# Moving three weight splits of GpSimd from ahead of the first expert gather to between the fourth and eighth

## The reference, cut to what matters

```python
q = (ht @ w_query).astype(jnp.float32).reshape(t_, PEER_HEADS, 2, PEER_HALF)
s1 = jnp.einsum('thd,hkd->thk', q[:, :, 0], sub_keys_1)   # and s2 with the other half
v1, i1 = lax.top_k(s1, PEER_TOPK)
...
idx = jnp.take_along_axis(cand_idx, pos, axis=-1)
gate = jax.nn.softmax(top_s, axis=-1)
...
u_sel = jnp.take(expert_down, ib, axis=0)
act = jnp.einsum('tkd,td->tk', u_sel, hb)
w = gb * jax.nn.gelu(act, approximate=False)
v_sel = jnp.take(expert_up, ib, axis=0)
return jnp.einsum('tk,tkd->td', w, v_sel)
```

## Time and profile before

| What | Value |
|---|---|
| Median of 3 runs | 3589.9 us (3586.92 to 3591.99) |
| Profiled execution, its own time | 3589.78 us |
| Span of that execution in the trace | 3588.0 us |
| PE busy | 3245.0 us, 90% of the span |
| POOL busy | 2185.1 us, 61% |
| DVE busy | 1754.7 us, 49% |
| ACT busy | 1332.6 us, 37% |
| All transfers | 936.79 MB, mean 261 GB/s |

### The profile page before, as it was taken

One profiled execution on the slowest core, in us unless ns is written; L12 is line 12 of the kernel. 1 busy time (PEld: TensorE's weight loads), 2 busy tenths in 40 slices (PEclk: granted clock), 3 DMA queues, 4 the chain that ended last, 5 costly groups with the idle time before them and its releaser, 6 DMA issues.

```text
span 3588.0 us, 38848 instructions
## 1 busy us (share of the span) xinstructions
PE 3245.0 (90%) x13642; PEld 2303.8 (64%) x13642; DVE 1754.7 (49%) x2582; ACT 1332.6 (37%) x2038; POOL 2185.1 (61%) x1216
## 2 busy tenths in 40 slices
PE   9999999996787788777877789999999999999998
PEld 7888878874343234222322338888888888878887
DVE  7998264238666447544744552222232133335444
ACT  6777576442111011000100014444444444445553
POOL 2021767876445444455555537887788778878665
PEclk9999999998999999999999999999999999999999
DMA  7455545669999999999999985555554445555444
GB/s 229 134 151 143 168 147 162 211 197 366 419 419 420 421 418 420 421 420 421 421 417 421 417 345 194 175 173 170 169 175 170 171 168 178 172 184 173 150 145 169
DMA packets 232765, 936.79 MB, mean 261 GB/s; under 512 B 28176, under 2 KB 31248, under 8 KB 166032
## 3 DMA queue, kind: packets, MB, share of 16 engines
q0 software_dynamic: 76288, 538.74, 36.3%
q1 hardware_dynamic: 152848, 391.96, 33.3%
q10 hardware_dynamic: 3456, 3.77, 0.3%
HBM read 927.04 MB, written 2.10 MB: 259 GB/s over the span
## 4 chain that ended last, share of the span: by engine, by line
PE 65%; DMA 25%; DVE 5%; POOL 1%; issue 1%; DVEq 1%; ACT 1%; ACTq 0%; SPq 0%; POOLq 0%
PE products L675 41%; DMA arena<-peer_up_in,arena 22%; PE products L2185 8%; PE products L1540 6%; DMA arena<-peer_down_in,arena 3%; DVE arena L2140 1%; POOL arena L2131 1%; PE products L1210 1%; PE products L2747 1%; PE products L1316 1%; PE products L2709 1%; PE products L1233 1%; DVE weights_low L634 1%; DVE arena L2166 0%; PE products L1222 0%
## 5 line engine op out<-in xcount | busy, mean ns | idle before, releaser
L634 POOL TENSOR_TENSOR weights_low<-arena,weights_high 128x1024 fp32r<-128x1024 f32 x484 | 1187.2, 2461 | 370.6 <-ACT weights_high L622 324.5
L2185 PE MATMUL products<-arena 128*128 128x512 f32 x1984 | 936.9, 618 | 290.2 <-DMA arena<-peer_up_in,arena 234.4
L622 ACT ACTIVATE weights_high<-arena 128x1024 fp32r<-128x1024 f32 x604 | 637.8, 1059 | 979.8 <-PE products L675 949.9
L675 PE MATMUL products<-weights_high,input_high 128*128 128x512 f32 x2416 | 985.2, 408 | 14.9 <-DVE weights_low L634 13.3
L675 PE MATMUL products<-weights_low,input_high 128*128 128x512 f32 x2416 | 946.6, 392 | 0.0
L675 PE MATMUL products<-weights_high,input_low 128*128 128x512 f32 x2416 | 944.3, 391 | 0.0
L2185 PEld LDWEIGHTS products<-arena 128*128 128x128 f32 x1984 | 369.6, 195 | 839.3 <-issue 418.9
L2140 DVE SCALAR_TENSOR_TENSOR arena<-arena 128x2048 f32<-128x2048 f32 x256 | 585.8, 2292 | 519.7 <-DMA arena<-peer_down_in,arena 519.3
L2131 POOL DMA_INDIRECT arena<-peer_up_in,arena x256 | 389.1, 1520 | 522.4 <-PE products L2185 500.2
L675 PEld LDWEIGHTS products<-weights_high,input_high 128*128 128x128 f32 x2416 | 455.8, 189 | 111.2 <-DVE weights_low L634 15.2
L675 PEld LDWEIGHTS products<-weights_low,input_high 128*128 128x128 f32 x2416 | 454.8, 188 | 98.7
(11 more groups left out here) (367 smaller groups left out, 3070.5 us busy)
## 6 DMA issues: line engine op xcount, KB each, us to landing
arena<-dsa_in SPq DMA_DIRECT2D x320, 512.0 KB, 3.5
arena<-w_in_in SPq DMA_DIRECT2D x128, 512.0 KB, 3.9
arena<-mla_wide_in SPq DMA_DIRECT2D x88, 512.0 KB, 3.5
arena<-w_attn_o_in SPq DMA_DIRECT2D x32, 512.0 KB, 4.3
arena<-w_out_in SPq DMA_DIRECT2D x32, 512.0 KB, 4.0
arena<-peer_w_query_in SPq DMA_DIRECT2D x32, 512.0 KB, 10.1
arena<-dsa_w_out_in SPq DMA_DIRECT2D x32, 512.0 KB, 3.8
arena<-glu_w_b_in SPq DMA_DIRECT2D x16, 512.0 KB, 3.7
```

The costliest lines, as they stand in the source:

```text
L622: nc.scalar.activation(w_hi[:, u % RING, :, at], ring[:, u % RING, :, at], ACT.Copy).then_inc(hi_made, 1)
L634: ops.tensor_tensor(w_lo[:, u % RING, :, at], ring[:, u % RING, :, at], w_hi[:, u % RING, :, at].bitcast(F32), op=ALU.subtract).then_inc(l ...
L675: mm = nc.tensor.matmul(PS[:, bank(b) + t, 0:width], x[:, x0 + n, at], y, start=n == 0 and m == 0, stop=n == len(parts) * PK - 1 and m == 2)
L2185: mm = nc.tensor.matmul(PS[:, SUM_BANKS[q]], diag[:, d % ROWS], row[:, q * NC:(q + 1) * NC], start=h % 2 == 0 and n == 0, stop=bool(last))
```

## The change

GpSimd no longer makes the low halves of parts 0 to 2 of the second query slab ahead of its first gather, nor that of part 3 after the fourth gather. It makes the one of part 0 after the fourth gather, of part 1 after the fifth, of part 2 after the sixth and of part 3 after the seventh.

```diff
             pool.wait_ge(lo_made, PARTS * (W_PQ + 1))
-            split_lo(pool, nc.gpsimd, W_PQ + 1, 0, range(RING - 1))
             pool.wait_ge(h2_ready, 1)
             pool.wait_ge(parts_used, PARTS * (W_PQ + 1))
             for kind, h, n in ROW_ORDER:
                 if kind == "down" and (h == 0 and n == TOPK // 2 or n == 0 and (h < 3 or h % 4 == 0)):
                     pool.wait_ge(experts_ready, experts_of(h, n))
                 load_row(pool, kind, h, n)
-                if (kind, h, n) == ("down", 0, RING - 1):
-                    split_lo(pool, nc.gpsimd, W_PQ + 1, 0, [RING - 1])
+                if (kind, h) == ("down", 0) and RING - 1 <= n < 2 * RING - 1:
+                    split_lo(pool, nc.gpsimd, W_PQ + 1, 0, [n - RING + 1])
```

## The result

The changed kernel takes 3599.69 us (median of 7 runs, 3599.39 to 3603.83), the kernel before on the same chips 3589.08 us (7 runs, 3586.92 to 3591.99). The ratio is 1.0031, with a 95% interval of 1.0022 to 1.0040: 10.6 us or 0.3% slower, and the interval lies wholly above 1. The profiled execution took 3600.69 us.

A forecast was written before the change was run, and what follows sets the result against it. Taken as bound by the gather flow's bytes, its start set by DVE's chain of dots. DVE's first low half +12.3 us, the 2.4 gain included, on 3589.8 gives 3602.1 us; range 3595 to 3608.

The forecast's parts named there:

- The path: From GpSimd's low halves through part 7's load, DVE's first low half and dots to the seventeenth gather: 12.3 us later.
- The sum: DVE's first low half at 848.3 in place of 835.98: +12.3 us, gain of 2.4 included, 3602.1 us; chance 0.57.
- rival of even turns: Loads of parts 4 to 7: each waits for one gather, 3.75 us a load; +8.7, 3598.5 us; chance 0.15.
- The landing: Last load (part 7) in the gathers' flow: lands at 847.2, after ten gathers and four loads; steps of 6.0 give 850.3.
- the gathers would run dry: Before DVE's first low half: only ten gathers can go, as the eleventh wants dot 2, behind DVE's wait.
- The choice of experts: Three tiny DVE instructions before the first gather: 0.20 us each, row numbers 3.9 us sooner, first gather 2.4 us sooner.
- Covered: From the eleventh gather on: queued gathers hide DVE's wait, only load bytes cost, 3.7 less 2.4: +1.3, 3591.1 us; chance 0.10.

The follow-up runs named there:

- narrower wait: Changed kernel, but DVE's first low half waits only for GpSimd's four low halves and its own high half, not all eight high halves: 3592.78 us, ratio 1.0008.
- second trace: The changed kernel run once more unaltered, for its trace alone; this execution took 3598.09 us.
- the two runs on the holes: Changed kernel with four second-head down rows gathered ahead of the first up row: 3598.38 us; the same, with DVE's first wait also cut: 3592.14 us.

## Why the prediction held

- **The path.** Seen as predicted at nearly each link: first gather 814.53 (814.4), GpSimd's first and fourth low half done at 821.73 and 832.39 (821.7 and 832.6), the last load landed at 847.05 (847.2), DVE's first low half at 848.16 (848.3), the seventeenth gather at 877.39 (877.6). The changed trace runs 0.44 us ahead of the other at L1020, so counted from there each of these came some 0.4 us later than forecast. The narrower wait shows that DVE's wait is the cause of most of the loss: without it, 6.9 of the 10.6 us between the medians come back, and the same edit gives nothing to the kernel before.
- **The sum.** Predicted +12.3, 12.6 in the first trace, 10.7 in the second, 10.6 between the medians. By the number alone the rival of even turns (3598.5) was nearer to 3599.7 than the forecast (3602.1); it is the path in the trace that speaks for the forecast. Two terms were over-sized a little. The landing was put at the end of ten gathers and four loads; in the second trace the last load comes out some 2 us ahead of it. And the loss was to be paid in full at the end; 1.7 and 1.1 us of it come back near 3260.
- **The landing.** The 6.0 us between loads held for the first two (833.5 and 839.7), then it fell to 3.9 and 3.5, because the ninth and the tenth gather had been issued late, at 838.19 and 840.75, behind dots 0 and 1. The queues of the changed kernel show it, 840 to 844 and 844 to 848:

```profile
q1 hardware_dynamic: 433, 0.82, 55.0%
q0 software_dynamic: 115, 0.81, 49.7%
```

```profile
q0 software_dynamic: 219, 1.60, 96.0%
q1 hardware_dynamic: 7, 0.01, 0.8%
```

First the loads have half of the flow. Then seven packets are all that their queue still moves, among the two late gathers, and the last load lands only at 847.05. In the second trace the load queue moves nothing more from 844 to 847, and the landing is 2 us sooner. So it is in part luck that 847.2 met 847.05. That the gathers would run dry was in the prediction; that they would thin out before was not. The running dry made little difference here: with the narrower wait the eleventh gather follows the tenth at once, and the last high half starts at 61.61 from L1020, against 61.03. Nor do bytes alone set this landing, as the prediction's sum had it: with the same bytes in larger pieces it came 4.7 us sooner.
- **The choice of experts.** The gain came: the three instructions take 0.17 to 0.18 us, and the first gather is 1.86 us sooner (2.4 forecast). What I bounded at 9.7 us, that DVE's second choice is held up beside GpSimd's low halves in turn, came to more than the change gave. L2062, L2024 and L2029 take 2.30, 3.04 and 3.14 us there, in place of 0.23, 0.18 and 0.43 in the kernel before, and each ends within 0.3 us behind the end of one of GpSimd's low halves (821.73, 828.85 and 832.39). Dot 0 is 4.06 us later, not sooner, so that DVE is idle from 839.6 and not from about 832. In the changed kernel this hides behind the wait; with the narrower wait it is what is left.
- **Covered.** The rival by which eight slots keep the flow fed fell to the windows: 10.2 us of idle time. The 3.7 us that it counts for bytes belong in the sums all the same: without them the two runs on the holes would fall short by that much more.
- **Turns.** That a load waits for just one gather (3.75 us) was my supposition in this rival; no row of the kernel before shows it. It is not what these loads do with pieces of 2 KB: the first two landings were 6.2 us apart, and in 826 to 834 the loads had a fifth of the bytes, in 350 packets beside 349. It is near what they do with pieces of 4 KB, which landed 3.75 us apart and had a third of the bytes, in 304 packets beside 302. In what order the packets of the two queues follow each other no run here shows, only that there were nearly as many from either.

## What to carry to other kernels

Low halves that free a slot are also the start of the next load, so before such work is moved behind something, look up where its loads would land and who waits for the last of them; a wait that covers more than its user needs costs nothing until then (the narrower wait left the kernel before at 3589.26 us beside 3589.03, and took 6.9 us off the changed one). In a stage that is bound by transfers, count what the transfer engines idle, hole by hole, and the bytes that are moved into it: in three kernels here that sum came within 0.5 to 1.7 us of the trace. Filling one hole sends the queue to the next row that it must wait for (here the twenty-fifth gather, which then waited 9.21 and 12.46 us for PE).

## What the runs showed of the hardware that was not expected

- Loads in pieces of 4 KB had a larger share of the full flow than loads in pieces of 2 KB. Among gathers in pieces of 8 KB, 512 KB in 256 pieces landed 6.0 to 6.2 us apart as long as gathers were queued, in 128 pieces 3.75 us apart; its queue had a fifth of the bytes in one case and a third in the other, with nearly as many packets as the gathers' queue in both (350 beside 349, 304 beside 302). The kernel before had the hint: its loads of dsa_in, in pieces of 4 KB (the loads' queue moves 0.53 MB in 148 packets in 1320 to 1340), landed in 7.8 to 8.6 us, at 420 GB/s in all. The trace of before for that tensor, 1300 to 1500:

```profile
DMA to landing us min/median/max: 7.8/7.9/8.6
```

- I had reckoned with DVE's type changes and shifts alone as what takes longer beside GpSimd's low halves. In the changed kernel a product of two inputs, L2029, takes 3.14 us beside GpSimd's low half of 829.99 to 832.39 (3.16 in its second trace), and 0.43 in the same form at 833.79. It ended at 832.67, just behind the low half, and by its record it had started 0.46 us ahead of it. The cast L2024 at 825.86 started within a gather's issue (825.50 to 826.46) and ended at 828.90, just behind the low half that came next (to 828.85). It took 3.04 us, in place of 0.18 in the kernel before.
